# Inverse roots that start from ScalarE's inverse root function instead of a square root and a reciprocal

## The reference

```python
def rms_norm(x, g):
    xf = x.astype(jnp.float32)
    y = xf * lax.rsqrt(jnp.mean(xf * xf, axis=-1, keepdims=True) + EPS)
    return (y * g.astype(jnp.float32)).astype(x.dtype)

# each layer of the first block
h_lat = rms_norm(x, norm_g[l]) * (1.0 + scale[:, None]) + shift[:, None]
q = rms_norm(q.reshape(B, S, GQA_HEADS, GQA_HEAD_DIM), q_gain)
k = rms_norm(k.reshape(B, S, GQA_KV_HEADS, GQA_HEAD_DIM), k_gain)
qm = (rms_norm(cq, cq_gain) @ w_uq)...       # rank 512
kvm = (rms_norm(ckv, ckv_gain) @ w_ukv)...   # rank 512
# each layer of the second block
kc = rms_norm_2(pc[..., k part].reshape(B, C, N_DIFF_HEADS, 2, DIFF_HEAD_DIM), k_norm_w)
attn_o = (rms_norm_2(o_attn, subln_w).reshape(B, L, D_ATTN) * (1.0 - lam_init) * jax.nn.silu(...))
```

## Time and profile before

| | before |
|---|---|
| time, median of 3 runs | 3085.9 us (3084.67 to 3092.2) |
| the profiled execution | 3091.4 us, span 3089.6 us, mean granted TensorE clock 0.976 |
| PE busy | 2924.8 us, 95% of the span |
| PEld busy | 2368.5 us, 77% |
| DVE busy | 1809.1 us, 59% |
| ACT busy | 1024.2 us, 33% |
| DVE RECIPROCAL of line 1072, the 30 large ones | 118.1 us |

### The profile page before, as it was taken

The page is one execution under the profiler, slowest core; times in us unless marked ns, Lnnn a source line. Parts: engine busy times, 40 slices in busy tenths (PEclk is TensorE's granted clock), DMA queues, the critical chain, the costliest instruction groups (busy, mean ns, idle before and its releaser), DMA issues.

```text
span 3089.6 us, 40874 instructions
## 1 busy us (share of the span) xinstructions
PE 2924.8 (95%) x16880; PEld 2368.5 (77%) x16880; DVE 1809.1 (59%) x2704; ACT 1024.2 (33%) x1513; POOL 109.4 (4%) x157
## 2 busy tenths in 40 slices
PE   6899999999998999999999989999999989999988
PEld 2587887776776878886777779767767778898888
DVE  3477677656336543465663576877564365738574
ACT  3222343324113233334332222335441132225453
POOL 0000000000000000000000000530000000004000
PEclk9999999999998999999999999999999989999999
DMA  9554344431445555634745345322644454322445
GB/s 405 216 188 140 130 150 143 148 149 44 173 170 187 196 193 184 222 106 160 280 164 192 132 147 184 106 93 89 218 157 170 170 189 139 99 94 89 160 155 171
DMA packets 136425, 501.92 MB, mean 162 GB/s; under 512 B 15024, under 2 KB 40368, under 8 KB 117552
## 3 DMA queue, kind: packets, MB, share of 16 engines
q1 hardware_dynamic: 126832, 489.64, 45.0%
q10 hardware_dynamic: 9408, 9.67, 0.9%
HBM read 484.05 MB, written 8.39 MB: 159 GB/s over the span
## 4 chain that ended last, share of the span: by engine, by line
PE 70%; DVE 11%; PEld 6%; issue 4%; DMA 4%; ACT 3%; SPq 2%; POOL 1%; PEldq 0%; DVEq 0%; ACTq 0%; POOLq 0%
PE products L1569 56%; PEld products L1569 5%; PE modulation L1667 3%; DVE tmp L1072 3%; DMA w_raw<-w_slots 2%; PE turned L1784 2%; PE scores L1767 1%; DVE w_low L1005 1%; DVE tmp L1118 1%; ACT w_high L668 1%; PE products L1747 1%; SPq L527 1%; DVE h_low L1146 1%; PEld turned L1784 1%; DMA mix_b<-ada_slots 1%
## 5 line engine op out<-in xcount | busy, mean ns | idle before, releaser
L1569 PE MATMUL products<-h_high,w_high 128*128 128x512 f32 (+1 forms) x3424 | 1253.2, 366 | 84.2 <-DVE w_low L1005 31.0
L1569 PE MATMUL products<-h_low,w_high 128*128 128x512 f32 (+1 forms) x3424 | 1192.8, 348 | 0.0
L1569 PE MATMUL products<-h_high,w_low 128*128 128x512 f32 (+1 forms) x3424 | 1191.8, 348 | 0.0
L1005 DVE TENSOR_TENSOR w_low<-w_raw,w_high 128x1024 fp32r<-128x1024 f32 x500 | 614.4, 1230 | 699.2 <-ACT w_high L668 695.4
L668 ACT CAST w_high<-w_raw 128x1024 fp32r<-128x1024 f32 x500 | 523.2, 1047 | 1375.9 <-PE products L1569 1203.9
L1569 PEld LDWEIGHTS products<-h_high,w_high 128*128 128x128 f32 x3424 | 660.6, 193 | 281.6 <-issue 139.5
L1569 PEld LDWEIGHTS products<-h_high,w_low 128*128 128x128 f32 x3424 | 660.5, 193 | 81.6
L1569 PEld LDWEIGHTS products<-h_low,w_high 128*128 128x128 f32 x3424 | 661.9, 193 | 78.4 <-issue 10.3
L1051 DVE SCALAR_TENSOR_TENSOR ada_w<-ada_w,cond_silu 128x1024 f32<-128x1024 f32 x180 | 224.6, 1289 | 1.1 <-DMA ada_w<-mod_slots 0.5
L1569 PE MATMUL products<-w_high,h_high 128*128 128x256 f32 x640 | 186.4, 291 | 13.3 <-DVE w_low L1005 12.8
L1569 PE MATMUL products<-w_high,h_low 128*128 128x256 f32 x640 | 184.4, 288 | 0.0
(11 more groups left out here) (223 smaller groups left out, 2660.9 us busy)
## 6 DMA issues: line engine op xcount, KB each, us to landing
w_raw<-w_slots SPq DMA_DIRECT2D x500, 512.0 KB, 3.5
ada_w<-ada_slots SPq DMA_DIRECT2D x122, 1024.0 KB, 7.8
ada_w<-mod_slots SPq DMA_DIRECT2D x96, 512.0 KB, 3.6
mix_a<-ada_slots SPq DMA_DIRECT2D x12, 1024.0 KB, 14.0
mix_b<-ada_slots SPq DMA_DIRECT2D x10, 1024.0 KB, 15.0
x_scratch<-x_residual ACTq DMA_DIRECT2D x3, 2048.0 KB, 7.8
x_residual<-x SPq DMA_DIRECT2D x1, 4096.0 KB, 14.2
x_residual<-x_scratch SPq DMA_DIRECT2D x2, 2048.0 KB, 10.0
```

The lines of the kernel that those rows point to most:

```text
L1005: nc.vector.tensor_tensor(wlo[:, n % SPL, :], raw[:, n % RAW, :], whi[:, n % SPL, :].bitcast(F32), ALU.subtract).then_inc(low_done, 1)
L1569: ins = nc.tensor.matmul(o, a, b, start=first and q == 0, stop=last and q == 2, skip_group_check=skip)
```

## The change

ScalarE's second activation gives the inverse root of the mean instead of the root, in all three places, and VectorE's reciprocal goes, with the wait for it. The Newton step stays as it is: it multiplies the mean by the estimate, then that by minus a half of the estimate, adds 1.5 and multiplies the estimate in.

```diff
             def mean_and_root(mean, root, src, inv):
 
                 nc.scalar.activation(mean, src, ACT.Identity, scale=inv, bias=eps_col[:, 0:1])
-                return nc.scalar.activation(root, src, ACT.Sqrt, scale=inv, bias=eps_col[:, 0:1])
+                return nc.scalar.activation(root, src, ACT.Abs_reciprocal_sqrt, scale=inv, bias=eps_col[:, 0:1])
...
             def root_table():
 
-                nc.scalar.activation(stat[:, 7, 3:4], eps_col[:, 0:1], ACT.Sqrt)
+                nc.scalar.activation(stat[:, 7, 3:4], eps_col[:, 0:1], ACT.Abs_reciprocal_sqrt)
...
             def x_root(layer):
...
                 act.wait_ge(x_var, layer + 1)
-                nc.scalar.activation(x_rs[:, 0:n], x_ms[:, 0:n], ACT.Sqrt).then_inc(x_rooted, 1)
+                nc.scalar.activation(x_rs[:, 0:n], x_ms[:, 0:n], ACT.Abs_reciprocal_sqrt).then_inc(x_rooted, 1)
...
             def inverse_begin(r, v):
-                step(nc.vector.reciprocal(r, r))
-                own()
                 step(nc.vector.tensor_tensor(v, v, r, ALU.mult))
```

## The result

The changed kernel takes 3048.55 us (median of 4 runs, 3043.52 to 3051.39), against 3089.05 us of the kernel before in the same runs: ratio 0.9872, 95% interval 0.9854 to 0.989, 40.5 us faster. The forecast was 3043 us and 42.5 us won; it had set out from 3085.9 us for the kernel before, 3.1 us less than the median here. The profiled execution took 3051.4 us.

What follows compares the result with a forecast made beforehand. TensorE, busy 95% of the span, was taken as the bound, so VectorE's work counts only where TensorE waits. Terms summed to 42.5 us, from a median of 3085.9 to 3043 us; own range 3030 to 3056, 8 in 10 3022 to 3068.

Steps and rivals of the forecast that it cites:

- The price of ScalarE's side: ScalarE's inverse root replaces Sqrt over the same tile: 0 taken for its duration and 0 for added table loads.
- (c): Rival: the new table set lacks Square alone; 28 loads, 36 us, no change that can be told, 3079 us; chance 0.06.
- (d): Rival: the table set lacks Copy too; 42 new loads, 54 us, slower by 11 us, 3097 us; chance 0.06.
- The places: Stretches in layers 0 to 3 where TensorE stalls behind a large reciprocal: eight terms, from 1.3 to 12.8 us.
- the first rank of layer 0: TensorE stalls of 0.73 and 0.53 us, both behind a reciprocal of 3.35 us: 1.3 us won.
- the k heads of layer 3: Four heads with five TensorE waits, the longest 1.61 us, each shorter than the reciprocal: 4.0 us won.
- the fourth k head of layer 2: Three waits and low clock behind it; VectorE dense, so gain capped at the reciprocal, 6.6 us; other bound 11.7.
- The clock term: Matmul time lost at low granted clock behind a stall, counted back where the stall goes entirely: 8.5 us in all.
- The dropped limits: Layer 2's last norm gains 1.3 us, not 3.4, because of the Silu; layer 1's second rank only its reciprocal, 3.4.
- down to about 15 us: Sign of being right: TensorE's waits for low parts of weight slots fall from 48 to about 15 us.
- Rival (a): The stalls go, but other waits stand right behind them: 27 us won, about 3059 us; chance 0.24.
- Rival (b): More comes back, at layer 2's fourth head (11.7 us) and in low-clock stretches: 55 us, 3031 us; chance 0.06.

Runs made afterwards that it cites:

- two-by-two: Two variants of the changed kernel: Sqrt back without a reciprocal, ratio 0.9864 to the kernel before; inverse root kept with a reciprocal at all 38 places, 0.9998.
- e3: The changed kernel with the reciprocal put back (of the mean, values wrong) in the ten k heads alone: 3074.54 us, ratio 0.9952 to the kernel before.
- e2: The changed kernel with a reciprocal of the same size put back at all 38 places (of the mean, values wrong): 3088.48 us, ratio 0.9998.

## Why the prediction was right

- **The price of ScalarE's side, nothing, held.** The inverse root runs as long as Sqrt, its set holds Copy, Square and Identity (no row has a load at their lines), and the two-by-two shows no time for the function. Rivals (c) and (d) fell with that. The Trainium skill ("ScalarE: Activation LUTs", "Table sets: the hidden batching unit") names cheap functions without Square; here Square ran without a load in this set too.
- **The places held, and the sum is closer than its terms.** 41.9 us were forecast against 42.3 us of lead, but that is in part luck: 2.8, 0.7 and 0.5 us too much at three places stand against 1.0, 1.3, 1.4 and 0.9 too little at others, and the norms of layer 3 give 6.6 to 9.5 us by the execution. The nine reciprocals without a stall cost nothing that the total shows for 28.6 us of VectorE, those in layer 3's norms 6.2 us for 14.0. TensorE's wait times, read off the timeline, were the right measure, VectorE's busy time was not.
- **Too small: the first rank of layer 0 (1.3, measured 2.3) and the k heads of layer 3 (4.0, measured 5.4).** The granted clock was 1.00 at both places before and after, so this isn't clock. Each wait was worth 0.25 to 0.3 us more than its idle time in the profile. Around layer 0's rank the lead steps by 1.0, 0.8 and 0.4 us, where the view of waits has 0.73 and 0.53 and no third; the five waits of layer 3 sum to 4.0 shown and 5.4 in lead, 0.28 each.
- **Too large: the fourth k head of layer 2 (6.6, measured 3.8 in this trace).** Before it, the first three gave 7.5 us against 6.2. The step that failed is "here VectorE is dense", from which the cap at the whole reciprocal came: without the reciprocal VectorE stands 2.72 us for ScalarE's cast, and only the rest comes through.
- **The clock term held where the stall went entirely** (layer 0: 3.4 us counted, 6.0 of 6.5 in lead). Of 8.5 us counted, layer 0, layer 1's k head and the first heads of layer 2 gave theirs, 6.8 us. In layer 3's norms 1.7 was counted and 3.4 came back, but in four of the other five traces with the same code there only 1.7 or none did. Mean granted clock 0.976 before, 0.980 after, which is about 74 and 61 us of matmul time lost.
- **The dropped limits held**: the Silu behind layer 2's last norm, and layer 1's second rank at exactly its reciprocal.
- **Wrong: TensorE's waits for low parts "down to about 15 us".** They fell from 48.1 to 35.0:

```profile
PE products L1567 <- DVE w_low L1005: 35.0, 16, 5.8
```

I had taken nearly all of them for root stalls. The waits that the prediction listed are 23.8 of the 48.1 us; the other half never stood behind a reciprocal (the longest, 5.8 us, is the same in both traces). At these places and in layer 3's norms 9.4 us are left or new: 1.04, 1.28, 1.04, 0.79, 3.73 and 1.49.
- **Rival (a) was half there.** Other waits did stand behind the old ones, VectorE's for the cast beside layer 2's fourth head and TensorE's in layer 3's norms, but they took about 4 us (2.8 short in the fourth head, 1.5 in the norms), not 15. Rival (b) wasn't: the fourth head came nowhere near 11.7 us, and the clock further on didn't rise.

## What to carry to other kernels

When an operation goes from an engine that isn't the bottleneck, walk through the bottleneck's own idle rows and ask of each whether that operation stands before it; the engine's busy time tells nothing of the worth (here nothing measurable per microsecond at one set of places, 0.44 at another). Cap each stall by the operation's length, ask what else the waiting instruction needs (here a Silu, a cast), and add the matmul time at low clock only where the stall goes entirely, as a chance and not as a sum. Where a result releases both a queue and a computation, as the scaled k here, look at both before the queue is reordered.

## What the runs showed of the hardware

- **The inverse root function costs what Sqrt costs**: 1110 ns on 128x1024, 686 ns on 128x512, 473 ns on 128x256, table load 1283 ns. What it gives is coarse: the step behind it is needed (0.075 of the output, above).
- **A wait of TensorE cost 0.25 to 0.3 us more than its idle time in the profile**, at a granted clock of 1.00. At the first one of layer 0's rank the waiting matmul moved by 0.89 us where 0.73 is shown, and the next by another 0.11, since the first row behind a wait lasts longer (0.50 against 0.39 us). The profile's ends of matmuls are modelled, which would explain the other 0.16; no run shows it.
- **The lead over the n-th matmul repeats to 0.1 us** between kernels at five of the places, where the runs of one kernel spread by 8 us. At places with a low clock or a wait for a load it doesn't: 3.8 to 5.7 and 6.6 to 9.5 us.
- **The same stall brings the low clock or doesn't.** At layer 1's k head stalls of 2.30 and 2.36 us were followed by 0.79 granted over 8 us (the kernel before and `e3`), one of 2.31 by 1.00 (`e2`), and whole executions of one program differ in it too (mean granted clock 0.975 to 0.979 over the twelve of `e2`).
